# Rows of two activation buffers placed 520 elements apart instead of 512

## The chip, the cores and the metric

The kernel runs on one NeuronCore of a Trainium2 chip. Its engines work side by side and meet only at semaphores: TensorE (PE in the profile, with its weight loads listed apart as PEld), VectorE (DVE), ScalarE (ACT), GpSimd (POOL), and the SyncE queue (SP), which issues the DMAs here. The metric is the time of one execution on the device in microseconds (us). A profiled execution gives the trace. TensorE's clock has two levels, 1.2 and 2.4 GHz; the profile gives the granted clock as a share of the higher one.

## The reference

Two residual layers over a sequence of 256 positions with 2048 channels, then an RMSNorm. What costs time is a set of dense products in float32:

```
hn = rms_norm(x, norm_w)                       # (256, 2048)
u  = hn @ w_in + b_in                          # 2048 x 20496 per layer
q, k, v, o, z_a, gates, glu_a, glu_b, z_b, g_a, g_b = split(u)
ya = mlstm(silu(conv5(q, k)), v, gates) gated by o, z_a
y_a = ya @ w_a                                 # 2048 x 2048
c  = glu_a * sigmoid(glu_b);  c = silu(layer_norm(conv31(c))) * silu(z_b)
y_b = c @ w_b                                  # 2048 x 2048
x  = x + (sigmoid(g_a)*y_a + sigmoid(g_b)*y_b) @ w_out
```

After both layers the output is `rms_norm(x, final_norm_w)`.

## The kernel before, in words

Everything stays in the on-chip memory (SBUF) with channels on the 128 partitions: a row of 2048 channels is 16 tiles (`KT`) of 128 channels by 256 positions. Products are taken in the float32r type, which TensorE streams faster than plain float32, and each operand is split into a high part (rounded to float32r) and a low part (the remainder). A product is then high x high, high x low and low x high.

Two buffers hold the activations that are multiplied. `Hs` (line 123) has 16 rows per partition, one per channel tile; a row is 512 elements: 256 positions of the high part and behind them 256 of the low part. `YC` (line 124) is built alike, for the branch outputs that go into `w_a` and `w_b`. Both are allocated as `[P, KT, 2 * S]`, so that a row begins 512 elements (2048 bytes) behind the one before.

Weights come in blocks of 2048 x 256 (a "pair" of output tiles), each in four chunks (`QC`) of four channel tiles (`KQ`). The SP queue loads a chunk into the ring `RAW` (lines 294 to 300), ScalarE rounds it into the high half of the ring `W` (`split_hi`, line 389), VectorE subtracts to make the low half (`split_lo`, line 690), and TensorE multiplies it. Four chunk slots are in flight. This order is written out by hand; no scheduler or pool decides anything.

The main product is `multiply` (lines 1240 to 1260). For each of the 16 channel tiles it issues what is called a quad below: two matmuls at line 1255 that stream the whole row of 512 elements (high and low) of `Hs` or `YC` against two high weight tiles, and two at line 1258 that stream the first 256 elements against the two low weight tiles. Each matmul has its own weight load of 128 columns. `multiply_turned` (lines 1262 to 1278, lines 1274 and 1276 in the profile), used for the v projection, has the roles swapped: a part of a row of `Hs` is the stationary operand and `W` streams (512 and then 256 elements).

The first 32 KiB of memory behind `Hs` are `YC`, then `RAW`, `W` and the rest, in the order of lines 122 to 146.

One more use: `GS` (line 155) is a view of the first eight rows of `YC` as 16 pieces of 256 elements. It holds the small gate weights, high part in elements 0 to 15 and low part in elements 128 to 143 of a piece. GpSimd clears it at the start (line 348), ScalarE and VectorE fill it at the start of each layer (lines 458 and 765), and TensorE uses it as the stationary operand in 32 matmuls of a layer (lines 1334 and 1335).

Of the kernel before, what the change touches and what calls it, by code (L numbers as in the profile page):

```python
# [30 lines left out]
F32 = mybir.dt.float32  # L31
F32R = mybir.dt.float32r
# [4 lines left out]
P = 128  # L37
L = 2
D = 2048
S = 256  # L40
ST = S // P
KT = D // P
# [4 lines left out]
DW_TAPS = 31  # L47
PAD = DW_TAPS // 2
CW = S + PAD
EPS = 1e-6  # L50
NG = 4 * H
GATE0 = 5 * D
# [59 lines left out]
def build_trunk(nc, x, norm_w, w_in, b_in, qk_conv_w, mlstm_norm_w, w_a, dw_w, dw_b,  # L112
                ln_w, ln_b, w_b, w_out, final_norm_w, out):
    with ExitStack() as ctx:
        def sb(name, shape, dt=F32):
            return ctx.enter_context(nc.sbuf_tensor(name, shape, dt))

        def sem(name):
            return ctx.enter_context(nc.semaphore(name))


        X = sb("X", [P, KT, S])
        Hs = sb("Hs", [P, KT, 2 * S], F32R)
        YC = sb("YC", [P, KT, 2 * S], F32R)
        RAW = sb("RAW", [P, QC, KQ, PC])
        W = sb("W", [P, QC, 2, KQ, PC], F32R)
        CP = sb("CP", [P, KT * CW + PAD])
        M = sb("M", [P, KT, S])
# [23 lines left out]
        KV_ = K_  # L152
        GW = HEAD[:, 2 * HT, :].rearrange("p (k g) -> p k g", k=KT)

        GS = YC[:, 0:KT // 2, :].rearrange("p k (a g) -> p (k a) g", a=2)
        GLOW, GATES = HEAD[0:NG, 2 * HT + 1, :], HEAD[0:NG, 2 * HT + 2, :]
        F_R, A_R, I_R, G_R, C_R, CB_R, Z_R, N_R = (HEAD[0:2 * H, i, :] for i in range(8))
        RS = EW[0:2 * H, 0:2, :]
# [32 lines left out]
        gs_clear = sem("gs_clear")  # L191
# [66 lines left out]
        def conv_in(tile, tap):  # L258

            return CP[:, ds(tile * CW + tap, S)]  # L260

        def conv_out(tile, count):

            return CP[:, tile * CW:(tile + count) * CW].rearrange(
                "p (t c) -> p t c", c=CW)[:, :, PAD:CW]

# [4 lines left out]
        def buf(g):  # L271

            return (EW, QB)[g % 2]
# [66 lines left out]
        @block.gpsimd  # L340
        def _(pool):
            steps = Steps(pool, pool_steps)
            steps.mark(nc.gpsimd.memset(IDENT[:], 0.0))
            steps.wait()
            nc.gpsimd.affine_select(out=IDENT[:], in_=IDENT[:], compare_op=ALU.not_equal, fill=1.0,
                                    base=0, pattern=[[-1, P]], channel_multiplier=1
                                    ).then_inc(ident_made, 1)
            nc.gpsimd.memset(YC[:, 0:KT // 2, :].bitcast(F32), 0.0).then_inc(gs_clear, 1)
            steps.mark(nc.gpsimd.memset(GC[:], 0.0))
            steps.mark(nc.gpsimd.memset(QPAD[:], 0.0))  # L350
            pool.wait_ge(rows_turned, 1)
            steps.mark(nc.gpsimd.memset(CP[:, 0:KT * CW].rearrange("p (t c) -> p t c", c=CW)
                                        [:, :, 0:PAD], 0.0))
            steps.mark(nc.gpsimd.memset(CP[:, KT * CW:], 0.0))
            steps.wait()
            pool.sem_inc(pads_made, 1)
            with pool.Fori(0, L) as l:

                n0 = pool.snap(l * NP)
                for c in range(QC):  # L360
                    pool.wait_ge(hi_made, n0 * QC + (c + 1))
                    nc.gpsimd.tensor_tensor(out=WL[:, c, :, :], in0=RAW[:, c, :, :],
                                            in1=WH[:, c, :, :].bitcast(F32), op=ALU.subtract
                                            ).then_inc(lo_made, 1)
                with pool.Fori(0, H) as h:
                    u = pool.snap(l * H + h)
                    pool.wait_ge(exp_made, u + 1)
                    pool.sem_inc(heads_seen, 1)
                    for d in range(2):

                        sign = 1 - 2 * d
                        w = EW[:, 2 * d:2 * d + 2, :]
                        nc.gpsimd.affine_select(out=w, in_=w, compare_op=ALU.is_ge, fill=0.0,
                                                base=0, pattern=[[-P * sign, ST], [sign, S]],
                                                channel_multiplier=-sign).then_inc(masked, 1)
                    pool.wait_ge(v_bias_in, u * 16 + 16)
                    pool.wait_ge(pairs_out, l * NP + h * 10 + (AT_HEAD + 8))
                    nc.gpsimd.tensor_tensor(out=VS, in0=VS,
                                            in1=VB.unsqueeze(1).to_broadcast([P, ST, DH]),
                                            op=ALU.add).then_inc(v_made, 1)  # L380
# [3 lines left out]
        def _(act):  # L384
# [63 lines left out]
            with act.Fori(0, L) as l:  # L448
# [8 lines left out]
                act.wait_ge(gs_clear, 1)  # L457
                nc.scalar.copy(GS[:, :, 0:NG], GW).then_inc(gw_hi, 1)

# [39 lines left out]
                with act.Fori(0, H) as h:  # L499
# [46 lines left out]
                    act.wait_ge(ya_made, u + 1)  # L546
                    nc.scalar.copy(YC[:, ds(h * HT, HT), 0:S], KV_).then_inc(ya_hi, 1)  # L547

# [36 lines left out]
                def cb_high(g):  # L585
                    act.wait_ge(cb_made, l * 4 + (g + 1))
                    nc.scalar.copy(YC[:, 4 * g:4 * g + 4, 0:S], buf(g)[:]).then_inc(cb_hi, 1)

# [94 lines left out]
        def _(dve):  # L683
# [19 lines left out]

            v.memset(EPSC[:], EPS)
            v.memset(ONES[:], 1.0).then_inc(ones_made, 1)
# [31 lines left out]
            with dve.Fori(0, L) as l:  # L737
# [21 lines left out]
                for p in range(KT // 2):  # L759
                    if p + 1 < KT // 2:  # L760
# [3 lines left out]
                dve.wait_ge(gw_hi, l + 1)  # L764
                v.tensor_tensor(GS[:, :, P:P + NG], GW, GS[:, :, 0:NG].bitcast(F32), ALU.subtract
                                ).then_inc(gw_lo, 1)
# [114 lines left out]
                with dve.Fori(0, H) as h:  # L881
# [145 lines left out]
                    for t in range(HT):  # L1027
                        if t % 2 == 0:
# [6 lines left out]
                    dve.wait_ge(ya_hi, u + 1)  # L1035
                    v.tensor_tensor(YC[:, ds(h * HT, HT), S:2 * S], KV_,
                                    YC[:, ds(h * HT, HT), 0:S].bitcast(F32), ALU.subtract
                                    ).then_inc(ya_lo, 1)
# [198 lines left out]
        def _(pe):  # L1237
# [86 lines left out]
            with pe.Fori(0, L) as l:  # L1324
# [8 lines left out]
                for k in range(KT):  # L1333
                    mm(px[:, 0, :], GS[:, k, 0:P], Hs[:, k, :], start=(k == 0), stop=False)  # L1334
                    i = mm(px[:, 0, S:2 * S], GS[:, k, P:2 * P], Hs[:, k, 0:S],
                           start=False, stop=(k == KT - 1))
# [156 lines left out]
```

## Time and profile before

| what | value |
|---|---|
| time, median of 3 runs | 2493.77 us (2492.16 to 2495.61) |
| profiled execution, its own time | 2491.69 us |
| its span | 2490.0 us |
| PE busy | 2455.4 us (99%), 14063 matmuls |
| PEld busy | 2141.2 us (86%) |
| DVE busy | 1934.5 us (78%) |
| ACT busy | 1317.2 us (53%) |
| POOL busy | 55.6 us (2%) |
| mean granted TensorE clock | 0.995 |
| DMA | 444.95 MB, mean 179 GB/s |

Busy time of matmuls is laid end to end in the page, and one matmul's duration includes its way through the array, so the mean of 397 ns of line 1255 is not what it costs in a row of matmuls. That is read from the distance of starts in the timeline. The 1.69 us between the span and the execution's own time lie outside the first and the last instruction.

### The profile page before, as it was taken

Reading aid. Unit: us, or ns where it says so; the run is one execution under the profiler, and the core shown is the slowest. Engines: PE = TensorE matmul, PEld = TensorE weight load, DVE = VectorE, ACT = ScalarE, POOL = GpSimd, SP = SyncE. Lnnn points to the kernel's source line nnn. Section 1 sums busy time; section 2 is a strip of 40 time slices with the busy share of each in tenths; the row PEclk is TensorE's granted clock in tenths of the full one; section 3 lists DMA queues with packets and bytes.
Section 4 is the critical chain, followed back from the end, with each engine's and each line's share of the span. In section 5 each row is a group of like instructions: output and inputs, shape, how many; then the busy total and the mean of one; then the engine's idle time right before and its main releaser. Section 6 shows DMA issues by size and latency. Waiting matters only on the chain.

```text
span 2490.0 us, 43931 instructions
## 1 busy us (share of the span) xinstructions
PE 2455.4 (99%) x14063; PEld 2141.2 (86%) x14063; DVE 1934.5 (78%) x2872; ACT 1317.2 (53%) x1574; POOL 55.6 (2%) x43
## 2 busy tenths in 40 slices
PE   7999999999999999999989999999999999999998
PEld 6888888888888888888878888888888888888887
DVE  5788989898988786556568888888888887765565
ACT  5545454545465557555354454545454655665543
POOL 2000000000000000000010000000000000000000
PEclk9999999999999999999999999999999999999999
DMA  6666656565656666665546655555565666666654
GB/s 186 178 187 181 183 161 184 165 181 165 181 177 187 191 181 189 189 188 190 171 128 188 194 178 175 172 177 173 170 181 158 190 188 186 178 196 191 185 186 135
DMA packets 447922, 444.95 MB, mean 179 GB/s; under 512 B 17968, under 2 KB 445760, under 8 KB 447808
## 3 DMA queue, kind: packets, MB, share of 16 engines
q1 hardware_dynamic: 447808, 443.74, 59.7%
q8 instruction: 34, 0.56, 0.1%
q14 instruction: 80, 0.66, 0.1%
HBM read 441.59 MB, written 2.10 MB: 178 GB/s over the span
## 4 chain that ended last, share of the span: by engine, by line
PE 95%; issue 2%; DVE 2%; ACT 1%; SPq 0%; DVEq 0%; DMA 0%; ACTq 0%
PE ps L1255 55%; PE ps L1258 27%; PE ps L1274 5%; PE ps L1276 2%; PE px L1414 1%; PE px L1393 1%; PE px L1320 1%; DVE Hs L751 0%; DVE HEAD L1030 0%; PE px L1384 0%; SPq L289 0%; PE px L1334 0%; ACT YC L547 0%; ACT W L389 0%; PE px L1401 0%
## 5 line engine op out<-in xcount | busy, mean ns | idle before, releaser
L1255 PE MATMUL ps<-Hs,W 128*128 128x512 f32 x5120 | 1617.7, 397 | 9.6 <-DVE Hs L751 9.6
L690 DVE TENSOR_TENSOR W<-RAW,W 128x1024 fp32r<-128x1024 f32 x824 | 1018.1, 1243 | 426.0 <-ACT W L389 420.4
L389 ACT CAST W<-RAW 128x1024 fp32r<-128x1024 f32 x832 | 866.5, 1048 | 905.3 <-PE ps L1258 795.1
L1258 PEld LDWEIGHTS ps<-Hs,W 128*128 128x128 f32 x5120 | 963.3, 188 | 227.9
L1258 PE MATMUL ps<-Hs,W 128*128 128x256 f32 x5120 | 1007.2, 278 | 0.0
L1255 PEld LDWEIGHTS ps<-Hs,W 128*128 128x128 f32 x5120 | 781.6, 189 | 15.2 <-DVE Hs L751 11.2
L792 DVE SCALAR_TENSOR_TENSOR ACC<-CP,CWT,ACC 128x256 f32<-128x256 f32 x928 | 388.1, 477 | 0.0
L1255 PE MATMUL ps<-YC,W 128*128 128x512 f32 x1024 | 321.6, 395 | 0.0
L1258 PEld LDWEIGHTS ps<-YC,W 128*128 128x128 f32 x1024 | 192.4, 188 | 45.5
L1258 PE MATMUL ps<-YC,W 128*128 128x256 f32 x1024 | 201.2, 278 | 0.0
L1274 PE MATMUL ps<-W,Hs 128*128 128x512 f32 x512 | 181.4, 399 | 0.0
L1255 PEld LDWEIGHTS ps<-YC,W 128*128 128x128 f32 x1024 | 155.9, 189 | 0.0
L1276 PE MATMUL ps<-W,Hs 128*128 128x256 f32 x512 | 142.8, 279 | 0.0
L402 ACT ACTIVATE T<-ps,PAR 128x256 f32<-128x256 f32 x288 | 120.0, 467 | 0.0
L1274 PEld LDWEIGHTS ps<-W,Hs 128*128 128x128 f32 x512 | 96.1, 188 | 22.6
L1276 PEld LDWEIGHTS ps<-W,Hs 128*128 128x128 f32 x512 | 96.4, 188 | 0.2
L697 DVE TENSOR_TENSOR QB<-ps,T 128x512 f32<-128x512 f32 x112 | 76.5, 683 | 0.6 <-ACT T L398 0.6
L906 DVE SCALAR_TENSOR_TENSOR HEAD<-QPAD,PAR,HEAD 128x256 f32<-128x256 f32 x128 | 58.2, 524 | 0.2
L446 ACT ACT_TABLE_LOAD x42 | 53.9, 1283 | 0.8
L906 DVE SCALAR_TENSOR_TENSOR QB<-QPAD,PAR,QB 128x256 f32<-128x256 f32 x128 | 52.8, 479 | 1.4 <-DVE QB L906 1.4
L389 ACT ACT_TABLE_LOAD x38 | 48.8, 1283 | 0.7
L446 ACT ACTIVATE QB<-QB 128x512 f32<-128x512 f32 x48 | 30.4, 632 | 18.9 <-DVE QB L697 18.5
(179 smaller groups left out, 978.7 us busy)
## 6 DMA issues: line engine op xcount, KB each, us to landing
RAW<-in_w_in_dram SPq DMA_DIRECT2D x640, 512.0 KB, 3.7
RAW<-in_w_a_dram SPq DMA_DIRECT2D x64, 512.0 KB, 3.3
RAW<-in_w_b_dram SPq DMA_DIRECT2D x64, 512.0 KB, 3.4
RAW<-in_w_out_dram SPq DMA_DIRECT2D x64, 512.0 KB, 4.0
M<-in_x_dram SPq DMA_DIRECT2D x2, 1024.0 KB, 8.4
HEAD<-in_b_in_dram SPq DMA_DIRECT2D x8, 256.0 KB, 3.8
out_dram<-M SPq DMA_DIRECT2D x4, 512.0 KB, 2.7
CP<-in_dw_w_dram SPq DMA_DIRECT2D x3, 128.0 KB, 4.7
```

Of the source, the lines that this page charges most:

```text
L389: nc.scalar.copy(WH[:, c, :, :], RAW[:, c, :, :]).then_inc(hi_made, 1)
L402: i = nc.scalar.activation(T[:, q, t, :], ps[:, 2 * q + t, S:2 * S], ACT.Identity, bias=bias(t))
L446: nc.scalar.activation(where, where, ACT.Sigmoid).then_inc(done, 1)
L690: v.tensor_tensor(WL[:, c, :, :], RAW[:, c, :, :], WH[:, c, :, :].bitcast(F32), ALU.subtract).then_inc(lo_made, 1)
L697: v.tensor_tensor(dst, ps[:, 2 * q:2 * q + 2, 0:S], T[:, q, :, :], ALU.add).then_inc(pairs_out, 1)
L792: steps.mark(v.scalar_tensor_tensor(out=dst, in0=src, scalar=w, in1=ACC[:, t, :], op0=ALU.mult, op1=ALU.add))
L906: ins = v.scalar_tensor_tensor(out=dst[:, t, :], in0=src, scalar=w, in1=dst[:, t, :], op0=ALU.mult, op1=ALU.add)
L1255: mm(ps[:, 2 * q + t, :], WH[:, c, kk, t * P:t * P + P], act_in[:, kt, :], start=(kt == 0), stop=False)
L1258: i = mm(ps[:, 2 * q + t, S:2 * S], WL[:, c, kk, t * P:t * P + P], act_in[:, kt, 0:S], start=False, stop=(kt == KT - 1))
L1274: mm(bank, Hs[:, kt, s * P:(s + 1) * P], W[:, c, :, kk, :], start=(kt == 0), stop=False)
L1276: i = mm(bank[:, 1, :], Hs[:, kt, S + s * P:S + (s + 1) * P], W[:, c, 0, kk, :], start=False, stop=(kt == KT - 1))
L1320: i = mm(px[:, bank, at + s * P:at + (s + 1) * P], columns[:, s:s + 1].to_broadcast([P, P]), IDENT[:], start=True, stop=True)
```

## The change

Both buffers get eight more elements per row and are then viewed without them, so that a row still shows 512 elements but begins 520 elements (2080 bytes) behind the one before. `GS` can no longer be eight contiguous rows cut in two; it becomes the first 256 elements of all 16 rows, and the clearing memset follows it. The two paddings are 16 x 8 x 4 = 512 bytes per buffer, so `YC` begins 512 bytes and `RAW`, `W` and all that follows 1024 bytes further on: the weight rings remain at multiples of 64 bytes. The number, kind and order of instructions on every engine stay the same; the memset has another shape (16 x 256 instead of 4096).

```diff
@@ -47,6 +47,7 @@
 PAD = DW_TAPS // 2
 CW = S + PAD
+ROW_PAD = 8
 EPS = 1e-6
@@ -120,8 +121,8 @@
         X = sb("X", [P, KT, S])
-        Hs = sb("Hs", [P, KT, 2 * S], F32R)
-        YC = sb("YC", [P, KT, 2 * S], F32R)
+        Hs = sb("Hs", [P, KT, 2 * S + ROW_PAD], F32R)[:, :, 0:2 * S]
+        YC = sb("YC", [P, KT, 2 * S + ROW_PAD], F32R)[:, :, 0:2 * S]
         RAW = sb("RAW", [P, QC, KQ, PC])
         W = sb("W", [P, QC, 2, KQ, PC], F32R)
@@ -152,7 +153,7 @@
-        GS = YC[:, 0:KT // 2, :].rearrange("p k (a g) -> p (k a) g", a=2)
+        GS = YC[:, :, 0:S]
@@ -345,7 +346,7 @@
-            nc.gpsimd.memset(YC[:, 0:KT // 2, :].bitcast(F32), 0.0).then_inc(gs_clear, 1)
+            nc.gpsimd.memset(GS.bitcast(F32), 0.0).then_inc(gs_clear, 1)
```

## Rows read from the trace of the kernel before

**Rows 1.** The page: span, busy time by engine, and the chain that ended last.
```profile
span 2490.0 us, 43931 instructions
...
PE 95%; issue 2%; DVE 2%; ACT 1%; SPq 0%; DVEq 0%; DMA 0%; ACTq 0%
```
**Rows 2.** Groups: line, engine, operation, tiles, shapes, count | busy us, mean ns | idle before.
```profile
L1255 PE MATMUL ps<-Hs,W 128*128 128x512 f32 x5120 | 1617.7, 397 | 9.6 <-DVE Hs L751 9.6
...
L1255 PE MATMUL ps<-YC,W 128*128 128x512 f32 x1024 | 321.6, 395 | 0.0
...
L1274 PE MATMUL ps<-W,Hs 128*128 128x512 f32 x512 | 181.4, 399 | 0.0
```
**Rows 3.** Timeline of PE, 1200.0 to 1203.6 us: start us, us, what, count.
```profile
1200.02 0.63 PE L1255 MATMUL ps<-Hs,W 128*128 128x512 f32 x2
1200.48 0.40 PE L1258 MATMUL ps<-Hs,W 128*128 128x256 f32 x2
1200.71 0.63 PE L1255 MATMUL ps<-Hs,W 128*128 128x512 f32 x2
...
1203.50 0.40 PE L1255 MATMUL ps<-Hs,W 128*128 128x512 f32 x1
```
**Rows 4.** Stretches: PE, PEld, DVE, ACT, POOL busy (instructions), granted clock, DMA share, GB/s.
```profile
820.00:920.00 100.00, 100.00 (x575) 87.27 (x574) 82.58 (x108) 55.22 (x63) 0.00 (x0) 1.00 0.61 183
1000.00:1100.00 100.00, 100.00 (x577) 87.25 (x576) 55.96 (x55) 56.56 (x62) 0.00 (x0) 1.00 0.62 188
...
```
**Rows 5.** The same view, 24.8 to 26.6 us.
```profile
24.80:26.60 1.80, 1.51 (x6) 1.02 (x5) 1.80 (x4) 0.29 (x1) 1.80 (x2) 0.50 0.18 30
```
**Rows 6.** Timeline of PE, 26.6 to 27.5 us (rows that reach into it).
```profile
26.14 0.63 PE L1255 MATMUL ps<-Hs,W 128*128 128x512 f32 x1
26.57 0.44 PE L1258 MATMUL ps<-Hs,W 128*128 128x256 f32 x2
26.84 0.62 PE L1255 MATMUL ps<-Hs,W 128*128 128x512 f32 x2
27.30 0.40 PE L1258 MATMUL ps<-Hs,W 128*128 128x256 f32 x2
```
**Rows 7.** Timeline of the weight loads, 26.5 to 28.5 us.
```profile
27.08 0.41 PEld L1258 LDWEIGHTS ps<-Hs,W 128*128 128x128 f32 x2
28.34 0.30 PEld L1255 LDWEIGHTS ps<-Hs,W 128*128 128x128 f32 x2 [0.85 <-DVE Hs L751]
```
**Rows 8.** Timeline of PE, 272 to 277 us: the turned product.
```profile
271.73 0.39 PE L1274 MATMUL ps<-W,Hs 128*128 128x512 f32 x1
...
272.07 0.40 PE L1274 MATMUL ps<-W,Hs 128*128 128x512 f32 x1
...
272.42 0.39 PE L1274 MATMUL ps<-W,Hs 128*128 128x512 f32 x1
```
**Rows 9.** Instructions on YC: duration ns min/median/max, first and last start us.
```profile
L1334 PE MATMUL px<-Hs,YC x32: 392/394/395, 38.2 to 1275.6; 128*128 128x512 f32 x32
...
L1079 DVE TENSOR_TENSOR YC<-EW,YC x4: 1215/1217/1221, 944.8 to 2199.1; 128x1024 fp32r<-128x1024 f32 x4
...
L458 ACT CAST YC<-HEAD x2: 401/402/402, 35.2 to 1267.4; 128x256 fp32r<-128x256 f32 x2
L765 DVE TENSOR_TENSOR YC<-HEAD,YC x2: 419/420/421, 35.9 to 1268.1; 128x256 fp32r<-128x256 f32 x2
L348 POOL MEMSET YC<- x1: 3512/3512/3512, 1.5 to 1.5; 128x4096 f32 x1
```
**Rows 10.** Groups on VectorE that touch neither buffer.
```profile
L1109 DVE TENSOR_TENSOR EW<-EW,QB 128x1024 f32<-128x1024 f32 x6 | 7.3, 1218 | 0.2
```
**Rows 11.** Waits of POOL: who waited for whom, us in total, times, longest.
```profile
POOL CP L352 <- PE ps L1296: 11.1, 1, 11.1
```
**Rows 12.** Waits: the ring on ScalarE, and ScalarE's own longest wait for a load.
```profile
ACT W L389 <- PE ps L1258: 795.1, 525, 6.5
...
ACT W L389 <- DMA RAW<-in_w_in_dram: 5.3, 6, 1.0
```

## The prediction, made before the changed kernel was run

> **What bounds the kernel now.** I read the page first: of a span of 2490.0 us the chain that ended last is 95% PE [rows 1]. No engine but TensorE sets the time. The ring of weights confirms it from the other side: ScalarE waited 795.1 us for slots that TensorE was still reading, and 5.3 us for loads [rows 12]. A change of layout can therefore matter in one way only: through the distance at which TensorE's matmuls follow each other.
>
> So the second view is the timeline of a calm stretch. The unit is a quad, two matmuls of 512 streamed elements and two of 256. Quads start at 1200.02, 1200.71 and so on to 1203.50 [rows 3]: five quads in 3.48 us, 0.696 us each. Inside one, two 512s take 1200.02 to 1200.48, 0.23 us each, and two 256s 1200.48 to 1200.71, 0.115 us each. The groups give the number of quads: (5120 + 1024 + 512) / 2 = 3328 [rows 2]. 3328 x 0.696 = 2316 us, so 93% of the span is this one pattern, and one ns of a quad is worth 3.3 us.
>
> The third view asks whether a quad holds time that a layout could give back. At 26.14 us the granted clock is 0.50 [rows 5], the level of 1.2 GHz, and a matmul of 512 elements is followed by the next after 26.57 - 26.14 = 0.43 us [rows 6]. At 2.4 GHz that would be 0.215 us if everything scaled with the clock; it is 0.23. A quad is three times 512 elements, 3 x 0.215 = 0.645, against 0.696. There are thus some 51 ns in each quad, 170 us in the whole kernel, that appear only at the higher clock. Either the streaming operand is delivered no faster than this wherever it lies, or it collides with something, and then addresses count.
>
> The fourth view tells against a collision with other engines. From 820 to 920 us VectorE is busy for 82.58 us, from 1000 to 1100 us for 55.96; TensorE has 575 and 577 instructions in them [rows 4], equal to within the two that stick out at the edges. The weight loads are the other suspect. After the pair of line 1258 that starts at 27.30, the next weight load comes at 28.34 [rows 6, 7], so the last of the two streamed with no load under it. The pair lasted 0.40 us, as long as the one at 1200.48 that had loads under both [rows 3]. The ends of matmuls are modelled, so this is weak evidence, but it points the same way.
>
> The fifth is the turned product. There `W` streams and `Hs` is stationary, with other row distances and other offsets between the two. Its quads are two of the steps 271.73, 272.07, 272.42 [rows 8]: 0.69 us, the same. Where the streaming row lies and how far the next row is has thus been varied within this kernel, with no effect. One thing has not: every row of `Hs`, `YC` and `W` begins at the same place within 512 bytes, since all sizes and steps are multiples of 512 bytes.
>
> **The change part by part.**
>
> Row distance of `Hs` and `YC`. No instruction is added, removed or moved; each of the 3072 quads of `multiply` reads the same number of elements from rows that now start 32 bytes further on, row by row, within a block of 512. A row is still contiguous. Bounds: at best all of the 51 ns go, -170 us; at worst each odd row, which now begins in the middle of a block of 64 bytes, touches one block more. A 512 is 32 such blocks in 0.232 us, 7.25 ns a block; four matmuls of a quad, half of the quads: 4 x 7.25 x 1536 = +45 us. I take 0, by the nearest rows: the same rate in the two forms of the product [rows 3, 8] and in the gate product, whose 512s have the duration of all others, 394 ns, with `YC` as the stationary operand at steps of 1024 bytes [rows 9].
>
> The rings moved by 1024 bytes. Their places within 64 and within 512 bytes stay as they are, and so do those of all later tensors. Cost 0; the bounds of the first item cover it.
>
> Writes into the padded rows. VectorE's low parts already write four separate pieces of 256 elements: 1217 ns [rows 9], against 1218 ns for a contiguous operation of the same size [rows 10]. A step between pieces costs nothing measurable, and 520 is only another step. 0, and were it 10% on VectorE, the waits of the ring would hide it.
>
> `GS`. The cast and the subtraction take 402 and 420 ns and start at 35.2 and 35.9 us; the gate product first runs at 38.2 [rows 9]. The subtraction ends near 36.3, which leaves 1.9 us. Even if both took twice as long (+0.8 us), they would be hidden. In the gate product itself the stationary pieces are still 128 contiguous elements: 0.
>
> The memset. 3.5 us on GpSimd from 1.5 us on [rows 9]. Twice the time, the most I can make of 16 pieces instead of one, would be +3.5 us; behind it GpSimd waits 11.1 us for TensorE's first transposes [rows 11], so it is hidden. Without that cover it would cost these 3.5 us once.
>
> Sum: 0 + 0 + 0 + 0 + 0. On the profiled execution that is 2491.69 us. The median of the runs shown is 2.1 us above it (the span is 1.69 below), so I state the forecast for the median: 2493.5 us.
>
> **What the skill says, weighed.** The trace shows the excess over the clock in quads with and without a weight load beneath [rows 3, 6, 7]. The Trainium skill, page "SBUF — State Buffer", section "Who interferes with whom", gives TensorE two read ports, one for the moving operand and one for LDWEIGHTS, independent of each other. By that rule the relative position of `Hs` and `W` can't matter, and the sum stays 0; the trace agrees as far as it goes. By the page "TensorE: Matmul & The Clock Gate", section "Back-to-back issue gap", a gap is N/2.4 + 2.5 ns, by which a quad would be an estimated 650 ns; then 46 ns of a quad, 153 us in all, would be the most that a better layout could return. No 512 at the higher clock in this trace comes that close.
>
> **Rivals.**
>
> Faster, because the two reading streams of TensorE meet in phase. For it: 51 ns of a quad that the lower clock doesn't show, and all rows at one place within 512 bytes, so that moving and stationary operands always begin in phase; 16 rows times 32 bytes would spread them over just that block. Against: the weights' offset to the moving row changes by 512 and 1024 bytes from tile to tile without a trace of it, the pair without a load beneath is not shorter, and the streams run at different speeds, so they'd leave the phase on their own. Price: between nothing and 170 us; if half of the excess goes, -85 us, 2409 us. Small parts of it would be seen as well, since 2 ns of a quad are 6.7 us.
>
> Slower, because rows lose their alignment to 64 bytes. Place: lines 1255 and 1258 on odd channel tiles. Price as above, up to +45 us, 2539 us; it decides from one extra access of more than 1 ns per matmul on (4 x 1 x 1536 = 6 us). For it: no unaligned row has ever been read in this trace, so nothing excludes it. Against: nothing in the rows names a block of 64 bytes.
>
> The change doesn't do what it says. The slice keeps the row distance of the allocation, so the addresses do move; that this is undone somewhere I hold for nearly impossible, and it would give no change, the same number as my forecast.
>
> **How the numbers follow.** No change (within 0.2% or 5 us, about what a measurement of this kernel can tell): 0.57, own range 2489 to 2499. Faster by phase: 0.24, spread from 2320 to 2488. Slower by alignment: 0.19, spread from 2499 to 2540. The range takes the forecast (0.57), the whole slower case (0.19) and the small end of the faster one (about 0.05): 2465 to 2540, 0.81 together.
>
> **What would show it.** In the changed profile, the distance of quads in a calm stretch of lines 1255 and 1258: 0.696 us again if I am right; below 0.69 for the phase rival, in all stretches alike and with the turned product moving too; above 0.70 for the alignment rival, and then alternating, quads of odd tiles longer than those of even ones, with the turned product (which streams `W`) unchanged. The durations of VectorE and ScalarE on `Hs` and `YC` should stay within a few ns, the memset should end before GpSimd's 11 us wait. I am wrong if the count of TensorE instructions in 100 us moves from 576 by more than 2.

## The result and the profile after

The changed kernel takes 2505.13 us (median of 4 runs, 2504.82 to 2506.74), against 2493.51 us (2492.16 to 2495.61) before: a ratio of 1.0047, 95% interval 1.003 to 1.0065. It is slower by about 11.6 us. The forecast was no change.

The page of the changed kernel: its span, its chain, and from the groups those of the streaming matmuls (line numbers are one higher than before):

```profile
span 2505.0 us, 43931 instructions
...
PE 95%; DVE 2%; issue 2%; ACT 1%; SPq 0%; DVEq 0%; DMA 0%; ACTq 0%
...
L1256 PE MATMUL ps<-Hs,W 128*128 128x512 f32 x5120 | 1613.6, 396 | 8.7 <-DVE Hs L752 8.6
...
L1259 PE MATMUL ps<-Hs,W 128*128 128x256 f32 x5120 | 1022.5, 281 | 0.0
...
L1256 PE MATMUL ps<-YC,W 128*128 128x512 f32 x1024 | 320.1, 394 | 0.0
```

The chain is TensorE's as before [rows 1], and the counts are the same. The 512s are even a little shorter (396 ns against 397 [rows 2]); the 256s have become longer, 281 ns on average. Before:

```profile
L1258 PE MATMUL ps<-Hs,W 128*128 128x256 f32 x5120 | 1007.2, 278 | 0.0
```

What counts is the distance of starts. The timeline of PE, first 1005 to 1008 us, then 1199.6 to 1210.9 us, with one row for the two 512s that begin a quad:

```profile
1005.04 0.63 PE L1256 MATMUL ps<-Hs,W 128*128 128x512 f32 x2
...
1006.44 0.62 PE L1256 MATMUL ps<-Hs,W 128*128 128x512 f32 x2
...
1007.13 0.63 PE L1256 MATMUL ps<-Hs,W 128*128 128x512 f32 x2
...
1007.84 0.62 PE L1256 MATMUL ps<-Hs,W 128*128 128x512 f32 x2
```
```profile
1199.64 0.63 PE L1256 MATMUL ps<-Hs,W 128*128 128x512 f32 x2
...
1210.84 0.63 PE L1256 MATMUL ps<-Hs,W 128*128 128x512 f32 x2
```

From the first row of the second piece to the last there are 16 quads: 11.20 us, 0.700 us each, against 0.696 before [rows 3]. The first piece begins a product: its tiles 0 and 1 take 1.40 us, tile 2 takes 0.69, tile 3 takes 0.71. Quads of the same work now have different lengths, and the pattern returns after eight tiles, that is after 8 x 32 = 256 bytes of shift: medians over all products with `Hs` are 700, 699, 692, 703, 703, 701, 703, 699 ns for tiles 0 to 7, and the same eight, within 1 ns, for tiles 8 to 15. Before, the medians were 696 to 698 for every tile. 3072 quads x (700.0 - 696.7) = 10 us, and the distances of starts inside the turned products, waits left out, add up to 177.2 us where it was 175.5. Together that is 11.8 us, the size of the loss in the medians.

The other engines did not change. The stretches of [rows 4], and from the instructions on `YC` the gate product, the writes, the fill of the gate weights and the memset:

```profile
820.00:920.00 100.00, 100.00 (x572) 87.43 (x571) 82.45 (x113) 54.35 (x61) 0.00 (x0) 1.00 0.61 184
1000.00:1100.00 100.00, 100.00 (x573) 87.47 (x572) 54.74 (x54) 56.37 (x62) 0.00 (x0) 1.00 0.61 189
```
```profile
L1335 PE MATMUL px<-Hs,YC x32: 396/397/398, 38.5 to 1283.4; 128*128 128x512 f32 x32
...
L1080 DVE TENSOR_TENSOR YC<-EW,YC x4: 1216/1218/1219, 950.8 to 2211.6; 128x1024 fp32r<-128x1024 f32 x4
...
L766 DVE TENSOR_TENSOR YC<-HEAD,YC x2: 419/419/419, 36.2 to 1275.8; 128x256 fp32r<-128x256 f32 x2
L349 POOL MEMSET YC<- x1: 3511/3511/3511, 1.5 to 1.5; 128x4096 f32 x1
```

TensorE does 572 and 573 instructions in 100 us instead of 575 and 577. VectorE's 1218 and 419 ns and the memset's 3511 ns are those of [rows 9] within 1 ns.

The profiled span grew by 15.0 us and the median by 11.6. One stretch of the profiled execution explains a part: from 80 to 90 us, after the small transposes of line 1365, the granted clock was 0.83 and TensorE did 55 instructions; before, 1.00 and 64. Nine instructions at a mean distance of 0.696 / 4 = 0.174 us are some 1.6 us. After and before:

```profile
80.00:90.00 10.00, 10.00 (x55) 8.80 (x54) 5.50 (x15) 4.74 (x6) 0.00 (x0) 0.83 0.49 145
```
```profile
80.00:90.00 10.00, 10.00 (x64) 8.87 (x63) 7.22 (x17) 5.81 (x7) 0.00 (x0) 1.00 0.52 153
```

### The profile page after: what moved, and what is told of

Read it like the earlier page. It is cut to its first block, busy times and chain, and to the rows that moved or that the text cites. A ratio compares the mean times of both kernels' runs of the same rounds, so it can differ in the third digit from the quotient of the medians.

```text
span 2505.0 us, 43931 instructions
## 1 busy us (share of the span) xinstructions
PE 2472.6 (99%) x14063; PEld 2160.0 (86%) x14063; DVE 1935.7 (77%) x2872; ACT 1315.8 (53%) x1574; POOL 55.6 (2%) x43
## 4 chain that ended last, share of the span: by engine, by line
PE 95%; DVE 2%; issue 2%; ACT 1%; SPq 0%; DVEq 0%; DMA 0%; ACTq 0%
PE ps L1256 55%; PE ps L1259 28%; PE ps L1275 5%; PE ps L1277 2%; PE px L1415 1%; PE px L1394 1%; PE px L1321 1%; DVE Hs L752 0%; DVE HEAD L1031 0%; PE px L1385 0%; SPq L290 0%; PE px L1335 0%; ACT YC L548 0%; ACT W L390 0%; PE px L1402 0%
## 5 line engine op out<-in xcount | busy, mean ns | idle before, releaser
L1259 PE MATMUL ps<-Hs,W 128*128 128x256 f32 x5120 | 1022.5, 281 | 0.0
```

What stands on the lines that cost most here:

```text
L1259: i = mm(ps[:, 2 * q + t, S:2 * S], WL[:, c, kk, t * P:t * P + P], act_in[:, kt, 0:S], start=False, stop=(kt == KT - 1))
```

## The experiments

In all of them "distance" means by how many bytes the rows of `Hs` and `YC` lie further on than the weight tiles, counted within 256 bytes, with the kernel before as 0. Quads are read as above: the starts of two 512s that are 16 quads apart, near 1200 us, so that 0.01 us in the start is 0.6 ns in a quad. That is one place of an execution; where another place has another pace, the text says so.

**Both buffers, everything, or W alone.** Three kernels with rows 512 elements apart as before, that only move whole buffers. The edits, shortened (gaps of elements, 4 bytes each; the second and third as comments):

```diff
 # buffers 64 bytes further on
+        sb("GAP_A", [P, 16])
         Hs = sb("Hs", [P, KT, 2 * S], F32R)
         YC = sb("YC", [P, KT, 2 * S], F32R)
+        sb("GAP_B", [P, 48])
         RAW = sb("RAW", [P, QC, KQ, PC])
 # everything 64 bytes further on: GAP_A of 16 ahead of Hs, GAP_C of 48 behind W
 # W alone 192 bytes further on: GAP_A of 48 ahead of W, GAP_C of 16 behind it
```

> Rows stay 512 elements apart; both activation buffers lie 64 bytes further on against the weight rings, and everything behind them is at its old place within 256 bytes. Theory A (the cost of a quad hangs on the distance between the streaming row and the stationary tile within 256 bytes): every quad of multiply behaves as the third and eleventh of the changed kernel, 692 ns instead of 696.6, so 3072 x -4.6 ns = -14 us, about 2479 us. Theory B (it hangs on where the streaming row itself begins within 256 bytes): the same here. Theory C (only rows that begin at 32 within 64 bytes are slower): 696.6 ns, 2493 us.

> Activation buffers and both weight rings all lie 64 bytes further on, so that their distance is as before; what lies behind W is at its old place within 256 bytes. Theory A: 696.6 ns a quad, 2493 us. Theory B: 692 ns a quad, 2479 us. Theory C: 2493 us.

> Only the ring W lies 192 bytes further on; the activation buffers have their old addresses, and what lies behind W its old place within 256 bytes. The distance within 256 bytes is that of the run with the buffers 64 bytes further on. Theory A: 692 ns a quad in multiply, 2479 us. Theory B: 696.6 ns in multiply (the streaming rows have not moved), 2493 us; the turned product, in which W streams, could change. Theory C: 2493 us.

Measured: 2477.82 us with the buffers moved (ratio to before 0.9938, interval 0.9921 to 0.9954), 2493.39 us with everything moved (1.0003, 0.9994 to 1.0013), 2477.42 us with `W` alone moved (0.9939, 0.9922 to 0.9955). The timelines of PE, in this order:

```profile
1199.85 0.62 PE L1257 MATMUL ps<-Hs,W 128*128 128x512 f32 x2
...
1210.89 0.62 PE L1257 MATMUL ps<-Hs,W 128*128 128x512 f32 x2
```
```profile
1199.64 0.62 PE L1257 MATMUL ps<-Hs,W 128*128 128x512 f32 x2
...
1210.78 0.62 PE L1257 MATMUL ps<-Hs,W 128*128 128x512 f32 x2
```
```profile
1200.10 0.62 PE L1257 MATMUL ps<-Hs,W 128*128 128x512 f32 x2
...
1211.13 0.62 PE L1257 MATMUL ps<-Hs,W 128*128 128x512 f32 x2
```

11.04, 11.14 and 11.03 us for 16 quads: 690, 696 and 689 ns. The third is the decisive one: the streaming rows have their old addresses, only the stationary operand has moved, and the matmuls are as fast as with the buffers moved. So at 64 bytes it is the distance of the two operands that counts, and not where a row begins. A's numbers (2479, 2493 and 2479 us) came out within 2 us; B fails on the second and third kernel, and C on the first and third, in which no row begins at 32 within 64 bytes and the time still moved. The first and the third kernel also beat the kernel before, by 0.6%.

**The gate weights and the memset alone.** The view `GS = YC[:, :, 0:S]` and its memset, with rows 512 apart.

> Rows 512 apart as before; only the view for the gate weights and its memset are those of the change. Every theory: the same as before, 2493 us, within 1 us. A gap of more than 2 us would mean that the side of the change that I priced at nothing carries a part of the 12 us.

Measured: 2492.97 us, ratio 1.0004 (0.9994 to 1.0013). This side of the change costs nothing that can be measured.

**Rows 528 elements apart.** `ROW_PAD = 16` in the changed kernel.

> The change with 16 elements of padding instead of 8 (rows 2112 bytes apart), so that rows begin at 0, 64, 128 and 192 bytes within 256 in turn and never at 32 within 64. Theories A and B, by the quads of the changed kernel at these places (700, 692, 703, 703): mean 699.5 ns, +9 us, about 2502 us, with a pattern that repeats every four quads. Theory C: 2493 us.

Measured: 2506.94 us, ratio 1.0059 (1.0042 to 1.0075), slower than A said.

```profile
1199.90 0.64 PE L1256 MATMUL ps<-Hs,W 128*128 128x512 f32 x2
1200.61 0.62 PE L1256 MATMUL ps<-Hs,W 128*128 128x512 f32 x2
1201.31 0.62 PE L1256 MATMUL ps<-Hs,W 128*128 128x512 f32 x2
...
1211.13 0.63 PE L1256 MATMUL ps<-Hs,W 128*128 128x512 f32 x2
```

16 quads take 11.23 us, 702 ns each. No row begins at 32 within 64 bytes here, so alignment alone can't be what makes a padded kernel slow. And this kernel has the distances 0, 64, 128 and 192, of which 64 was just seen to be fast.

**What the 51 ns over the clock are.** In `multiply`, an operand or the width of the weight load depends on the tile, so this kernel leaves out a part of the products. The edit, shortened:

```diff
+ m = P if kt < 8 or kt == KT - 1 else P // 2 if kt < 12 else P // 4
+ big = act_in[:, kt, 0:1].to_broadcast([P, 2 * S]) if kt // 4 == 1 else act_in[:, kt, :]
- mm(ps[:, 2 * q + t, :], WH[:, c, kk, t * P:t * P + P], act_in[:, kt, :], ...)
+ mm(ps[0:m, 2 * q + t, :], WH[:, c, kk, t * P:t * P + m], big, ...)   # and line 1258 alike
```

> Leaves work out: in multiply, channel tiles 4 to 7 stream one element of the row over and over in place of the row, tiles 8 to 11 load only 64 weight columns, tiles 12 to 14 only 32; tiles 0 to 3 and 15 are as before. Where do the 51 ns of a quad over the clock come from? Theory D (a limit of the streaming read alone): tiles 4 to 7 fall to about 645 to 650 ns, tiles 8 to 14 stay near 697. Theory E (streaming reads and weight loads meet): tiles 8 to 11 lose about half of the excess, some 670 ns, tiles 12 to 14 three quarters, some 658; tiles 4 to 7 fall as well if the repeated element stays out of the loads' way. Theory F (the array or its output is the limit): no tile changes.

Measured, in one run: 2468.2 us. Rows for tiles 4 and 5 (one element repeated), 8 to 10 (64 columns), and 12 to 13 (32 columns):

```profile
1202.10 0.60 PE L1260 MATMUL ps<-Hs,W 128*128 128x512 f32 x2
...
1202.76 0.60 PE L1260 MATMUL ps<-Hs,W 128*128 128x512 f32 x2
...
1204.74 0.62 PE L1260 MATMUL ps<-Hs,W 128*64 128x512 f32 x2
...
1206.12 0.63 PE L1260 MATMUL ps<-Hs,W 128*64 128x512 f32 x2
...
1207.52 0.64 PE L1260 MATMUL ps<-Hs,W 128*32 128x512 f32 x2
...
1208.24 0.63 PE L1260 MATMUL ps<-Hs,W 128*32 128x512 f32 x2
```

The four quads that repeat an element begin at 1202.10 and end at 1204.74: 0.66 us each, 36 ns less. The next two take 0.69 each, tile 10 takes 0.70, and the first with 32 columns 0.72. Narrower loads save nothing. So most of the excess, 36 of some 51 ns, comes with a stream that advances through memory (theory D comes nearest, though 0.66 is not quite its 0.645 to 0.65), E's proportion to the load is refuted, and F falls. Whether such a stream is slow by itself or collides with the loads, tiles 4 to 7 do not tell: a repeated element might stay out of the loads' way as well. The distance of the weight tile nevertheless shifts the same stream by several ns either way.

**The other constant distances.** The edit of the first experiment with other gaps (for 48, both buffers are slices that begin 12 elements into a longer allocation).

> Rows 512 elements apart, both activation buffers 32 bytes further on against the rings; every row begins at 32 within 64 bytes. Theory A, from the second and tenth tile of the changed kernel: 699 ns a quad in multiply, about 2500 us. If the quads of the changed kernel also carry a debt from the tile before them, a constant distance need not give its number; then 690 to 705 ns. Theory C (odd rows are slow): over 703 ns, since all rows are odd.

> The same with 96 bytes. Theory A, from the fourth and twelfth tile of the changed kernel: 703 ns a quad, about 2512 us. Theory C: as with 32 bytes.

> The same with 128 bytes. Theory A, from the fifth and thirteenth tile: 703 ns a quad, about 2512 us. A period of 128 bytes would give 696.6 ns and 2493 us.

> The same with 192 bytes, the mirror image of the fast distance of 64. Theory A, from the seventh and fifteenth tile: 703 ns a quad, about 2512 us. If only the size of the distance counted and not which operand is ahead: 690 ns as with 64 bytes, about 2478 us.

> Rows 512 apart, buffers 160 bytes further on. The four distances measured so far average 696.1 ns with 192 and 128; if the changed kernel were simply the mean of its eight distances, 160 and 224 would have to average about 711 ns. Theory G: both are near 697 ns, about 2494 us. Theory A without any cost of steps: about 711 ns, some 2530 us.

> The same with 224 bytes, and the same two numbers: about 697 ns by theory G, about 711 ns if the mean of the distances is to explain the changed kernel.

> Rows 512 apart, buffers 48 bytes further on, between the distances of 32 (693.3 ns) and 64 (690.1 ns). A smooth dependence: about 691.7 ns, 2481 us. If reads go by blocks of 32 or 64 bytes, a start in the middle of one costs an access more per row: over 695 ns.

Each was run once, except 0 and 64; the kernel before, run beside them, took 2493.56 and 2494.22 us.

| distance, bytes | 16 quads, us | a quad, ns | time, us |
|---|---|---|---|
| 0 (before) | 11.14 | 696 | 2493.5 |
| 32 | 11.10 | 694 | 2482.9 |
| 48 | 11.20 | 700 | 2505.5 |
| 64 | 11.04 | 690 | 2477.8 |
| 96 | 11.30 | 706 | 2518.9 |
| 128 | 11.15 | 697 | 2493.5 |
| 160 | 11.26 | 704 | 2512.1 |
| 192 | 11.09 | 693 | 2483.7 |
| 224 | 11.24 | 702 | 2509.8 |

The slowest of them, 96 bytes, in the timeline:

```profile
1199.63 0.63 PE L1257 MATMUL ps<-Hs,W 128*128 128x512 f32 x2
...
1210.93 0.63 PE L1257 MATMUL ps<-Hs,W 128*128 128x512 f32 x2
```

One constant moves the kernel by 41 us, between 64 and 96. The dependence is not smooth (48 is slower than both 32 and 64) and not symmetric in any way I can name. Theory C is refuted as it stands: at 32 every row begins at 32 within 64 bytes, and the kernel is 10.6 us faster than the kernel before that ran beside it. A share of the alignment is not excluded, though. The other odd multiples of 32 (96, 160, 224) are the slowest of the table, and 48, the only start that is no multiple of 32, was expected over 695 ns on just that ground and took 700. `W` was moved alone for the distance of 64 and for no other, so only there are distance and place told apart. The single numbers that A took from the changed kernel's tiles were wrong as well: 699 was expected at 32 and came out as 694, 703 at 96, 128 and 192 as 706, 697 and 693. A tile's quad in the changed kernel is not the quad of its distance.

The mean of the eight distances that the changed kernel runs through (without 48) is 2496.5 us. The changed kernel takes 2505.1. About 3 us of its loss are the mean of its distances; the larger rest, some 9 us, is something else. It shows in the kernels in which the distance changes from row to row. The expectation for 160 and 224 named two numbers, 697 and 711 ns; 704 and 702 lie between them.

**One layout, two paces.** The distance does not fix the pace alone. In the run at 96 bytes the same addresses are read in every product, and the timeline holds two paces, one before four other matmuls and one behind them:

```profile
918.33 0.63 PE L1257 MATMUL ps<-Hs,W 128*128 128x512 f32 x2
...
928.83 0.63 PE L1257 MATMUL ps<-Hs,W 128*128 128x512 f32 x2
929.29 0.39 PE L1260 MATMUL ps<-Hs,W 128*128 128x256 f32 x2
929.52 1.03 PE L1307 MATMUL px<-EW,ONES 128*128 128x256 f32 x4
...
931.80 0.63 PE L1257 MATMUL ps<-Hs,W 128*128 128x512 f32 x2
...
943.11 0.63 PE L1257 MATMUL ps<-Hs,W 128*128 128x512 f32 x2
```

The first two rows are 15 quads apart, 700 ns each; the last two are 16 quads apart, 707 ns each (the 706 of the table). Of the 192 products of `multiply`, each of 16 quads, 12 have a wait or the lower clock in their second half; of the other 180, 32 run at 700 ns and 148 at 707. Without a wait or other matmuls in between the pace never changed, in one stretch through 462 quads. The other constant distances of the table show one pace each (at 224, 701 to 704 ns), and so do the kernels with rows 520 and 528 elements apart (700 and 702 ns).

**Rows in groups of four.** `Hs` is cut into four groups of four rows, 512 elements apart inside, each group 8 elements further on.

```diff
+ g = first // 4     # the group of the row
+ rows = hs_all[:, 8 * g + 2048 * g:8 * g + 2048 * (g + 1)].rearrange("p (k c) -> p k c", k=4)
```

> Rows of Hs 512 elements apart within groups of four tiles, the groups at 0, 32, 64 and 96 bytes; YC as before. The question is why the changed kernel's quads (mean 700 ns) are slower than those of constant distances (696.7, 693.3, 690.1, 706.6 for these four). Theory G (a row whose distance differs from the row before it pays for the step itself): quads 1 to 3 of a group settle at the four numbers, and the first quad of a group is longer by 4 ns or more. Theory H (the cost belongs to the row's own distance and the one before it does not count): all four quads of a group show the group's number from the first on.

Measured, in one run: 2497.47 us, beside 2494.22 before. The quads of tiles 4 to 11 of one product and the start of tile 12:

```profile
1004.17 0.63 PE L1267 MATMUL ps<-Hs,W 128*128 128x512 f32 x2
...
1004.87 0.63 PE L1267 MATMUL ps<-Hs,W 128*128 128x512 f32 x2
...
1005.58 0.62 PE L1267 MATMUL ps<-Hs,W 128*128 128x512 f32 x2
...
1006.27 0.62 PE L1267 MATMUL ps<-Hs,W 128*128 128x512 f32 x2
...
1006.96 0.63 PE L1267 MATMUL ps<-Hs,W 128*128 128x512 f32 x2
...
1007.67 0.63 PE L1267 MATMUL ps<-Hs,W 128*128 128x512 f32 x2
...
1008.37 0.62 PE L1267 MATMUL ps<-Hs,W 128*128 128x512 f32 x2
...
1009.06 0.62 PE L1267 MATMUL ps<-Hs,W 128*128 128x512 f32 x2
...
1009.75 0.63 PE L1267 MATMUL ps<-Hs,W 128*128 128x512 f32 x2
```

At 32 bytes: 0.70, 0.71, then 0.69 and 0.69. At 64 bytes: 0.71, 0.70, then 0.69 and 0.69. The first two quads after a step are long, and only then does the pace of the constant distance appear. That is what theory G says, with two quads where I had said one. The last group does not fit it in size: the medians of tiles 12 to 15, at 96 bytes, are 703, then 700 three times. They never reach the 706 of the table, but 700 is the other pace of the constant kernel.

**A step inside the quad.** Buffers at 64, and the low half of each weight slot 128 bytes further on.

```diff
-        W = sb("W", [P, QC, 2, KQ, PC], F32R)
+        W = sb("W", [P, QC, 2, KQ * PC + 32], F32R)[:, :, :, 0:KQ * PC].rearrange(
+            "p c h (k n) -> p c h k n", k=KQ)
```

> The buffers 64 bytes further on as in the fastest run, and besides the low half of each weight slot 128 bytes further on against the high half, so that the distance steps inside the quad: 64 for the two 512s, 192 (as 64 - 128) for the two 256s. Theory G (steps of the distance cost): slower than with one distance, 695 to 705 ns a quad, 2490 to 2520 us. Theory H (each matmul has the cost of its own distance): between the quads of 64 (690.1) and 192 (693.3), 692 ns, about 2483 us.

Measured: 2501.47 us, ratio 1.0032 (1.002 to 1.0043).

```profile
1199.75 0.63 PE L1258 MATMUL ps<-Hs,W 128*128 128x512 f32 x2
...
1211.01 0.63 PE L1258 MATMUL ps<-Hs,W 128*128 128x512 f32 x2
```

Here 16 quads take 11.26 us, 704 ns each, though the two distances alone give 690 and 693. But this is the slower of two paces. The same execution earlier, at the start of one product with `Hs` and of the next product, again 16 quads apart:

```profile
777.79 0.62 PE L1258 MATMUL ps<-Hs,W 128*128 128x512 f32 x2
...
788.88 0.62 PE L1258 MATMUL ps<-YC,W 128*128 128x512 f32 x2
```

11.09 us, 693 ns each. Of 180 products without a wait or the lower clock in their second half, 76 run at 693 ns and 104 at 703, and as at 96 bytes the pace changes only where waits or other matmuls come between. 693 is what theory H expected (692), so H is not refuted by this kernel, and G's cost of a step, if there is one inside the quad, is not always paid. The time of 2501.47 us is a mixture of the two. What stands against H is the row distance: the kernel with rows 528 apart holds 702 ns in every product, where its four distances alone average (696 + 690 + 697 + 693) / 4 = 694 ns.

## Why the prediction was wrong

**The bound** was right: TensorE's streaming matmuls set the time, a ns of a quad is worth about 3.3 us, and the loss came through the distance of starts and in no other way.

**The row distance, the first item of the sum, is the step that failed.** It was set to 0 "by the nearest rows": the same pace in the plain, the turned and the gate product. All of these have their operands at the same distance within 256 bytes, because every size was a multiple of 512 bytes. I had written that this alone had never been varied, and then took 0 from rows that could not show it. The item was +10 us in `multiply` and another 1.7 us in the turned product. By subtraction, about 3 us of the loss are the mean of the distances that the rows run through, and the larger rest comes with their change from row to row.

**The argument against the phase rival** had three parts. That the offset changes by 512 and 1024 bytes from tile to tile without effect is true and proves nothing, since these are multiples of 256. That two streams of different speed would leave a phase by themselves doesn't fit the runs: a pace is kept from product to product, 690 ns through the whole kernel at 64 bytes, and where there are two paces it changes only behind a wait or other matmuls. The pair of matmuls without a load beneath, called weak evidence, was weak. The rival's condition, the relative position of the two operands, is what the runs show to matter; its sign was wrong for this layout. I let it lead only to a gain, on the ground that spreading the phases must dissolve a conflict. In fact the distance of 0 is a middling one (four constant distances are slower, three faster, one equal), and walking through all of them came out slower than their mean.

**The alignment rival** gave a time on the right side (up to +45 us), but its mechanism as written is refuted: it wanted odd tiles long, even ones short and the turned product unchanged, and a layout with all rows at 32 within 64 bytes is faster than before. The measured 2505.13 us lies inside the stated range of 2465 to 2540 us only because of this rival's share of it, which is luck. The sign of being wrong did its work: TensorE's count in 100 us fell from 575 and 577 to 572 and 573, by more than the 2 from 576 that were allowed.

**The Trainium skill's rule** that TensorE's two read ports are independent (page "SBUF — State Buffer", section "Who interferes with whom") would have left the time alone whatever the distance. The measurement decides against that use of it: with `W` alone moved by 192 bytes the kernel is 14.6 us faster (2477.42 against 2492.01).

**The items at nothing** held as far as they were run: moving buffers and rings together by 64 bytes had no effect (the rings' own 1024 bytes were not run alone), the writes into padded rows stayed within 2 ns, and gate weights and memset together gave 1.0004. The gate product's own 512s took 3 ns more, 397 against 394 [rows 9], on 32 matmuls. The padding and its steps need not be the reason: with everything moved by 64 bytes, that is with rows, gate view and distance as before, they took 398:

```profile
L1336 PE MATMUL px<-Hs,YC x32: 395/398/403, 37.6 to 1275.3; 128*128 128x512 f32 x32
```

**Open.** The runs show that the row distance made the loss, that the relative place of the operands within 256 bytes sets the pace together with what ran just before, and that the excess belongs mostly to a stream that moves on. They don't show what in the memory or in TensorE does it, what picks one of two paces, whether the changed kernel's 700 ns is a cost of steps or a slow pace of that kind, why 64-column loads save nothing, or how much of the slow odd multiples of 32 is alignment. The single runs of the table carry about 2 us of scatter each; the differences named are larger.

## What to carry to other kernels

In a kernel bound by float32r matmuls, the distance between the streaming and the stationary operand is a tuning parameter: try constant shifts of one buffer by multiples of 32 bytes up to 256, since here they cost two lines and ranged over 41 us, with 64 bytes 0.6% faster than the layout that sizes had given by chance. Keep the distance the same from row to row; padding rows to "spread" it made things worse at two paddings, with and without 64-byte alignment. Judge a layout by the time of the whole kernel, or by quads from several places, since one layout can have two paces. And when all rows of a profile share one property, a pace that is the same everywhere is no evidence that the property doesn't matter.

## What the runs showed of the hardware that I had not expected

- The length of a float32r matmul in a dense sequence depends on where its weights lie against its streaming row: 690 to 706 ns a quad, and in the changed kernel a pattern that returns after 256 bytes of shift.
- With rows in groups of four, two quads of 0.70 to 0.71 us passed after the steps to 32 and to 64 bytes until the new pace of 0.69 was reached.
- The same addresses can be read at two paces: 700 or 707 ns a quad at 96 bytes, 693 or 703 with the low weights 128 bytes further on. A pace lasts until a wait or other matmuls break the sequence. In the kernel at 64 bytes even the gate product differs between the two layers: its 16 pairs of matmuls begin 346 ns apart on average in the first and 353 in the second.
- At the 2.4 GHz level a 512 that streams one element over and over is followed by the next after 0.22 us, as half of the 0.43 us at 1.2 GHz [rows 6] would have it; one that streams a row is followed after 0.23.
